# Two memories laid out by feature, parameters as one array, and the small inner products of eight units regrouped

## The chip, the cores and the metric

One core of a Trainium2 chip runs the whole program. The metric is the device time in microseconds (us) of one execution; the median of three runs stands for a kernel. TensorE (PE; its weight loads are PEld), VectorE (DVE), ScalarE (ACT), GpSimd (POOL) and SyncE (SP, which issues most DMAs) each run their own list of instructions in order and meet at semaphores.

## The reference

Two blocks of a sequence model, at batch 1, 256 tokens and 1024 features, all in float32. Block 1: an RMS norm and one wide projection feed a stick-breaking attention (sb), an mLSTM branch (ml) and a cross attention (xa) over 256 memory rows `mem`, whose norm is `mem * rsqrt(mean(mem^2)) * g_mem`; the gated outputs are merged and projected, and a convolved gated feed-forward follows. Block 2, two layers: a gated linear recurrence over 8 heads (hg, the part the change touches), a latent attention with rotary positions (mla), an attention over a second memory `mem_2` that is not normed, an output projection and a LayerNorm.

What the eight heads compute, in the form that the kernel uses: with `b` the running sum of the log forget gates,

```python
A[t, s] = sum_d q[t, d] * exp(b[t, d] - b[s, d]) * k[s, d]     # s <= t
o[t]    = sum_s A[t, s] * v[s]
```

The kernel forms `exp` of such differences about the midpoint of every node of a binary tree over the 256 tokens, so that each exponent is at most zero.

## The kernel before

Every float32 operand of a large product is split into an upper and a lower part. ACT copies a landed weight piece from `raw` (4 slots) to `whi` (6 slots, L1065), DVE subtracts to get `wlo` (L1538), and PE does three products for each tile: upper by upper, upper by lower, lower by upper (L589 to L591 where the output is by feature, L598 to L600 where it is by token). A piece is 512 KB of a weight matrix, 24 or 12 matmuls. Pieces stand in one list, and all engines go through it in order; `split_until(n)` in the ACT and DVE programs says up to which piece they split before their next other work, mostly six pieces ahead of PE. SP loads piece c when DVE has split piece c-4. `project(name, ...)` is PE's loop over the pieces of one matrix, `part` a range of them. The order of everything between pieces is written out by hand in each engine's program; there is no planner.

**The start.** SP loads the identity, `mem` in two row blocks, then pieces 0 to 3, then X. ACT issues 13 small DMAs of parameter vectors into staging rows. PE transposes three of these vectors (L675), DVE copies them to `cols1` (L1603), PE transposes `mem` in 16 tiles (`turn`, L634), ACT and DVE split the tiles from PSUM with the gain `g_mem` (`turned`, L1104 and L1559), and only then are the first weight pieces split and `xak`, the first projection, begins. The 16 transposes of the normed X come between `xak` and `xav`, those of the other parameters (L689 to L693) between `xav` and `xaq`. Row sums of squares of `mem` and X are ACT passes with an accumulator (L1154, L1160).

**The small constants.** After the evacuations of `xak` and `xav`, ACT copies the tree masks (L1179) and takes logs and sines (L1184, L1186), and DVE does some twenty-five small operations for the rotary angles (L1627 to L1654), before both go on with the pieces of `xaq`. In the attention of `xa`, DVE's `attend_shares` ends with the normed shares, ACT's `attend_turned` (L1117) copies their transposes, and PE's `attend_values` (L659) waits for these.

**The second memory.** `mem_2` is loaded twice by row block, each time transposed by PE in 16 tiles (before `out20`, and before `hgf0` of layer 0) and split by ACT and DVE tile by tile.

**The recurrence (in each of two layers).** Eight units u, two for each pair of heads. PE's `decays(u, ...)` sums logs through tree masks (L935, L936), ACT takes the exponential (`weights`, L1425), DVE multiplies keys and queries in (`factors`, four operations at L496), PE forms the inner products (`products`), DVE moves them into AT and AC (`keep`), and after an odd unit puts the diagonal blocks into AT (`diagonal`, L2027). Then PE can form the pair's outputs (`outputs`, L997, L998). An even unit has the levels of 128, 64 and 32 columns (L964, L968, L971) and level 3 in 32-column products (L979); an odd unit has levels 4 to 8, five levels in 32-column products (L979). `products(u-1)` stands in PE's program after `decays(u, 2, 4)`; a piece of `hgg` stands between `decays(u, 0, 2)` and `decays(u, 2, 4)`. After the last unit come `outputs(2)`, `products(7)`, a piece of `mlaout1`, `squares(2)` (L1004) and `outputs(3)`, which waits for DVE's `keep(7)`, `gated(2)`, `scaled(0)` and `diagonal(3)`.

**The end.** DVE adds the last projection to X by row block, takes its statistics, waits for ACT's square root, takes the reciprocal (L2094), then subtracts the mean and multiplies by the gain (L2095), and scales and adds (L2099).

## Time and profile before

| | us |
|---|---|
| median of three runs | 1051.24 (1051.14 to 1052.27) |
| profiled execution, its own time | 1052.53 |
| its span in the trace | 1050.7 |
| PE busy | 1030.6 |
| DVE busy | 730.9 |
| ACT busy | 654.1 |

The busy time of an engine is the union of its instructions. A matmul's end is modelled and overlaps the next one's start, so a PE that runs on steadily is seen best by the distance between starts, which is what the chain of waits prints. The mean granted clock over the span is 0.997. In the chain of waits the six projection lines have 13% of the span each, and PE as a whole has 95%.

### The profile page before, as it was taken

What the parts mean: (1) busy time and instruction counts of PE and PEld (TensorE: products, weight loads), DVE (VectorE), ACT (ScalarE), POOL (GpSimd) and SP (SyncE); (2) the same over time, 40 slices, a digit from 0 to 9 for tenths busy, and PEclk for the clock granted to TensorE, in tenths of its full rate; (3) what the DMA queues carried; (4) which work ended last, traced back from release to release, by engine and by line L of the source; (5) the groups of instructions that cost most, each with busy time, mean ns of one, the idle gap of its engine ahead of it and who ended that gap; (6) DMA issues with size and microseconds to landing.
All of it is one profiled execution on the core that took longest, in us unless ns stands there. A gap on an engine that the chain in (4) does not pass through costs nothing.

```text
span 1050.7 us, 19082 instructions
## 1 busy us (share of the span) xinstructions
PE 1030.6 (98%) x8048; PEld 922.0 (88%) x8048; DVE 730.9 (70%) x1085; ACT 654.1 (62%) x924; POOL 13.3 (1%) x18
## 2 busy tenths in 40 slices
PE   6999999999999999999999999999999999999996
PEld 5798987888989999988999998888799999988875
DVE  4684688885747788765565758977884656599686
ACT  6776576564456656544466678657755667776583
POOL 1000000000000000000000000100000000001000
PEclk9999999999999999999999999999999999999999
DMA  8663434666547655566544533422565455344231
GB/s 307 225 202 120 142 124 137 200 200 201 173 149 228 195 179 167 193 223 187 173 160 130 165 125 120 141 83 102 180 199 168 130 161 161 101 143 142 79 116 47
DMA packets 97831, 167.52 MB, mean 159 GB/s; under 512 B 7048, under 2 KB 32530, under 8 KB 97490
## 3 DMA queue, kind: packets, MB, share of 16 engines
q1 hardware_dynamic: 95776, 159.24, 47.3%
q0 software_dynamic: 1472, 5.51, 1.5%
q10 hardware_dynamic: 498, 1.55, 0.4%
q8 instruction: 63, 1.03, 0.4%
q14 instruction: 22, 0.18, 0.0%
HBM read 165.23 MB, written 1.05 MB: 158 GB/s over the span
## 4 chain that ended last, share of the span: by engine, by line
PE 95%; DVE 3%; DMA 1%; ACT 1%; issue 1%; SPq 0%; DVEq 0%
PE proj L598 13%; PE proj L589 13%; PE proj L600 13%; PE proj L599 13%; PE proj L591 13%; PE proj L590 13%; PE mix L935 1%; PE mix L979 1%; PE mix L936 1%; PE mix L634 1%; PE mix L659 1%; PE mix L642 1%; PE mix L968 1%; DVE wlo L1538 1%; DMA raw<-in_w_mem_kv 1%; PE mix L875 1%
## 5 line engine op out<-in xcount | busy, mean ns | idle before, releaser
L1538 DVE TENSOR_TENSOR wlo<-raw,whi 128x1024 fp32r<-128x1024 f32 (+3 forms) x303 | 355.4, 1202 | 139.9 <-ACT whi L1065 138.0
L1065 ACT ACTIVATE whi<-raw 128x1024 fp32r<-128x1024 f32 (+3 forms) x303 | 306.2, 1040 | 148.1 <-PE proj L600 66.5
L589 PE MATMUL proj<-act_hi,whi 128*128 128x256 f32 x1064 | 303.5, 285 | 0.6 <-ACT arena L1082 0.4
L591 PE MATMUL proj<-act_hi,wlo 128*128 128x256 f32 x1064 | 300.9, 283 | 0.0
L590 PE MATMUL proj<-act_lo,whi 128*128 128x256 f32 x1064 | 300.9, 283 | 0.0
L589 PEld LDWEIGHTS proj<-act_hi,whi 128*128 128x128 f32 x1064 | 203.1, 191 | 3.3 <-ACT arena L1082 1.2
L590 PEld LDWEIGHTS proj<-act_lo,whi 128*128 128x128 f32 x1064 | 203.2, 191 | 0.9
L591 PEld LDWEIGHTS proj<-act_hi,wlo 128*128 128x128 f32 x1064 | 203.2, 191 | 0.2
L598 PE MATMUL proj<-whi,y_hi 128*128 128x512 f32 (+1 forms) x340 | 135.1, 397 | 3.8 <-DVE wlo L1538 3.5
L599 PE MATMUL proj<-wlo,y_hi 128*128 128x512 f32 (+1 forms) x340 | 132.4, 389 | 0.0
L600 PE MATMUL proj<-whi,y_lo 128*128 128x512 f32 (+1 forms) x340 | 132.3, 389 | 0.0
L598 PE MATMUL proj<-whi,act_hi 128*128 128x512 f32 (+1 forms) x288 | 113.3, 393 | 0.0
L600 PE MATMUL proj<-whi,act_lo 128*128 128x512 f32 (+1 forms) x288 | 111.0, 386 | 0.0
L599 PE MATMUL proj<-wlo,act_hi 128*128 128x512 f32 (+1 forms) x288 | 110.9, 385 | 0.0
L598 PEld LDWEIGHTS proj<-whi,y_hi 128*128 128x128 f32 x340 | 64.3, 189 | 19.5 <-DVE wlo L1538 4.3
L600 PEld LDWEIGHTS proj<-whi,y_lo 128*128 128x128 f32 x340 | 64.3, 189 | 13.5
L599 PEld LDWEIGHTS proj<-wlo,y_hi 128*128 128x128 f32 x340 | 64.3, 189 | 12.7 <-issue 0.5
L598 PEld LDWEIGHTS proj<-whi,act_hi 128*128 128x128 f32 x288 | 54.1, 188 | 10.3 <-issue 0.5
L600 PEld LDWEIGHTS proj<-whi,act_lo 128*128 128x128 f32 x288 | 54.1, 188 | 10.2
L599 PEld LDWEIGHTS proj<-wlo,act_hi 128*128 128x128 f32 x288 | 54.1, 188 | 9.6
L1076 ACT ACTIVATE arena<-proj 128x1024 f32<-128x1024 f32 (+2 forms) x40 | 39.8, 996 | 36.4 <-PE proj L591 21.7
L496 DVE TENSOR_TENSOR arena<-arena 128x512 f32<-128x512 f32 x64 | 41.1, 703 | 25.9 <-ACT arena L1425 25.5
(360 smaller groups left out, 1239.7 us busy)
## 6 DMA issues: line engine op xcount, KB each, us to landing
raw<-in_w_in SPq DMA_DIRECT2D x144, 512.0 KB, 4.4
raw<-in_w_up SPq DMA_DIRECT2D x88, 256.0 KB, 4.2
raw<-in_w_out SPq DMA_DIRECT2D x32, 512.0 KB, 4.3
raw<-in_w_down SPq DMA_DIRECT2D x22, 512.0 KB, 5.4
raw<-in_w_mem_kv SPq DMA_DIRECT2D x8, 512.0 KB, 9.1
raw<-in_w_mem_k SPq DMA_DIRECT2D x8, 512.0 KB, 4.0
raw<-in_w_o SPq DMA_DIRECT2D x8, 512.0 KB, 3.7
raw<-in_w_mem_v SPq DMA_DIRECT2D x8, 512.0 KB, 3.9
```

The costliest lines, as they stand in the source:

```text
L496: return mul(z, z, kq, ALU.mult)
L589: mm(o, wh[:, i, wc], hi[:, k0 + i, :], start=begin and j % 2 == 0, stop=False, skip_group_check=True)
L590: mm(o, wh[:, i, wc], lo[:, k0 + i, :], start=False, stop=False, skip_group_check=True)
L591: last = mm(o, wl[:, i, wc], hi[:, k0 + i, :], start=False, stop=end, skip_group_check=True)
L598: mm(o, hi[:, k0 + i, tb], wh[:, i, :], start=begin, stop=False)
L599: mm(o, hi[:, k0 + i, tb], wl[:, i, :], start=False, stop=False)
L600: last = mm(o, lo[:, k0 + i, tb], wh[:, i, :], start=False, stop=end)
L634: last = nc.tensor.transpose(mix[:, k // 2, (k % 2) * SEQ + b * P:(k % 2) * SEQ + (b + 1) * P], src(k, b), ident)
L642: last = mm(mix[:, h, b * SEQ:(b + 1) * SEQ], q(h)[:, b * P:(b + 1) * P], k(h), start=True, stop=True)
L1065: fn(whi[c % SPLIT][:, 0:w], raw[c % SLOTS][:, 0:w], ACT.Copy).then_inc(s.w_hi, 1)
L1076: fn(dst, src, func).then_inc(out_of(name, L)[0], 1)
L1538: tt(wlo[c % SPLIT][:, 0:w], raw[c % SLOTS][:, 0:w], f32(whi[c % SPLIT][:, 0:w]), ALU.subtract).then_inc(s.w_lo, 1)
```

## The change

One diff with these parts. (1) On the host, arrays are laid out: `mem` and `mem_2` by feature, `[128, 8, 256]`, and all parameter vectors by column in one array `par`; the kernel loads `mem` in two halves of four feature tiles, and `par` in one DMA. (2) The transposes of `mem`, of `mem_2` (twice) and of the parameters are gone. ACT and DVE split `mem` straight from SBUF, and `mem_2` in one operation each. The sums of squares of `mem` are an ACT square, a DVE sum over the eight tiles, and two small matmuls with a vector of ones after `xak`. (3) The transposes of X stand between the second and third piece of `xav`. (4) The small constants move behind the first attention's exponentials. (5) The inner products: level 8 goes from the odd unit to the even one; an even unit is `outer_products`; an odd unit is `early_products` (levels 4, 5), which PE does a unit later between its two halves of `decays`, and `late_products` (levels 6, 7); for unit 7 the late ones come amid the piece of `mlaout1`. DVE copies the widest levels of an even unit (`keep_widest`) between the second and third of the odd unit's `factors`, and `early_products` wait for it. (6) In the last LayerNorm the subtraction comes ahead of the wait for the square root.

```diff
 # SP
-            sp.dma_start(const[:, 0:P], a["const"][:, 0:P]).then_inc(s.ident_in, 16)
-            for b in range(NB):
-                sp.dma_start(MEM[:, b, :], a["mem"][0, b * P:(b + 1) * P]).then_inc(s.mem_in, 16)
             for c, loads in enumerate(pieces):
-                if c == SLOTS:
+                if c in (0, 2):
+                    half = slice(c * KT // 4, c * KT // 4 + KT // 2)
+                    sp.dma_start(MEM[:, half, :], a["mem"][:, half, :]).then_inc(s.mem_rest if c else s.mem_in, 16)
+                if c == SLOTS + 1:
                     sp.dma_start(X[:, :, :], a["x"][0].rearrange("(b p) d -> p b d", p=P)).then_inc(s.x_in, 16)
...
 # PE, the start
+            project("xak", None, MEM_hi, MEM_lo, ready=lambda k: pe.wait_ge(s.mem_lo, k))
+            pe.wait_ge(s.mem_sum, 1)
+            for b in range(NB):
+                last = mm(mix[:, 3, 4 * b:4 * b + 4], MEM_SUM[:, b * P:(b + 1) * P], ONE4, start=True, stop=True)
+            last.then_inc(s.mem_ss, 1)
+            project("xav", None, MEM_hi, MEM_lo, part=(0, 2))
+            pe.wait_ge(s.norm_x, 1)
             pe.wait_ge(s.ident_in, 16)
...
-            turn(KT, lambda k, b: MEM[:, b, k * P:(k + 1) * P])
-            project("xak", None, MEM_hi, MEM_lo, ready=lambda k: pe.wait_ge(s.mem_lo, k))
-            pe.wait_ge(*stage(2, None))
-            pe.wait_ge(s.norm_x, 1)
-            turn(KT, lambda k, b: XN[:, b, k * P:(k + 1) * P])
-            project("xav", None, MEM_hi, MEM_lo)
...
 # PE, the second memory (the same in layer 0)
-            pe.wait_ge(s.mem2_in, 16)
-            turn(KT, lambda k, b: MEM2_AT[None][:, b, k * P:(k + 1) * P])
...
 # PE, the inner products
+                def outer_products(u):
+
+                    pe.wait_ge(s.hg_z, 32 * L + 4 * u + 4)
+                    if u:
+                        pe.wait_ge(s.hg_cp, 8 * L + u)
+                    else:
+                        pe.wait_ge(s.hg_ll, 4 * L + 4)
+                    inner(u, (8,))
...
+                    inner(u, (3,)).then_inc(s.hg_pr, 1)
+
+                def early_products(u):
+
+                    pe.wait_ge(s.hg_z, 32 * L + 4 * u + 2)
+                    pe.wait_ge(s.hg_outer, 4 * L + u // 2 + 1)
+                    inner(u, (4, 5))
+
+                def late_products(u):
+
+                    pe.wait_ge(s.hg_z, 32 * L + 4 * u + 4)
+                    pe.wait_ge(s.hg_cp, 8 * L + u)
+                    inner(u, (6, 7)).then_inc(s.hg_pr, 1)
...
                 for u in range(1, UNITS):
                     decays(u, 0, 2)
+                    if u % 2 == 0:
+                        early_products(u - 1)
...
-                    products(u - 1)
+                    if u % 2:
+                        outer_products(u - 1)
+                    else:
+                        late_products(u - 1)
...
+                early_products(UNITS - 1)
                 outputs(2)
-                products(UNITS - 1)
-                project("mlaout1", L, y_hi, y_lo, 8, part=(1, 2))
+                project("mlaout1", L, y_hi, y_lo, 8, part=(1, 2), amid=lambda: late_products(UNITS - 1))
...
 # ACT
+            act.dma_start(par[:, :], a["params"]).then_inc(s.params, 16)
+            act.dma_start(const[:, 0:P], a["const"][:, 0:P]).then_inc(s.ident_in, 16)
...
+            mem_upper(range(KT // 2))
+            split_until(2)
+            act.wait_ge(s.mem_rest, 16)
+            mem_upper(range(KT // 2, KT))
+            split_until(SLOTS)
+            fn(MEM_SQ, MEM, ACT.Square).then_inc(s.mem_sq, 1)
...
             attend_exp(0, XP, XA_D ** -0.5)
+            split_until(ahead_of("sbv", None, 1))
             act.wait_ge(s.tree_in, 16)
             fn(tree[:, :, :, :].rearrange("p b l t -> p (b l t)"), TREE_IN, ACT.Copy).then_inc(s.tree_ok, 1)
...
-            turned("mem2", None, KT, MEM_hi, lambda k: 1.0)
+            act.wait_ge(s.mem2_in, 16)
+            fn(MEM_hi, MEM2_AT[None], ACT.Copy).then_inc(s.mem2_hi, 1)
...
 # DVE
+                    stt(MEM_lo[:, k, :], MEM[:, k, :], cols1[:, 1, k:k + 1], f32(MEM_hi[:, k, :]), ALU.mult, ALU.subtract).then_inc(s.mem_lo, 1)
...
                     for i in range(4):
-                        last = halves(tt, u, i)
-                    last.then_inc(s.hg_z, 1)
+                        if u % 2 and i == 2:
+                            keep_widest(u - 1)
+                        halves(tt, u, i).then_inc(s.hg_z, 1)
+
+                def keep_widest(u):
+
+                    heads = slice(u, u + 2)
+                    dve.wait_ge(s.hg_pr, 8 * L + u + 1)
+                    if u == 0:
+                        dve.wait_ge(s.hg_zero, L + 1)
+                    copy(AT[:, heads, P:SEQ], mix[:, 2, 0:SEQ].rearrange("p (h t) -> p h t", h=2))
+                    copy(both(AT[0:64, heads, 64:P], SEQ, 64), mix[0:64, 2, SEQ:512].rearrange("p (h b t) -> p h b t", h=2, b=2)).then_inc(s.hg_outer, 1)
...
+                        link(masked(3, mix[:, 3, P:2 * P]))
+                        last = masked(8, mix[:, 3, 2 * P:3 * P])
...
+                    stt(x, x, stat[:, 72 + 2 * b:73 + 2 * b], LNG, ALU.subtract, ALU.mult).then_inc(s.ln_s, 1)
                     dve.wait_ge(s.ln_r, 2 * L + b + 1)
                     nc.vector.reciprocal(r, r).then_inc(s.ln_s, 1)
-                    stt(x, x, stat[:, 72 + 2 * b:73 + 2 * b], LNG, ALU.subtract, ALU.mult).then_inc(s.ln_s, 1)
```

## Rows read from the trace of the kernel before

**Rows 1.** the page's busy times: engine, us busy, share of the span, instructions.

```profile
PE 1030.6 (98%) x8048; PEld 922.0 (88%) x8048; DVE 730.9 (70%) x1085; ACT 654.1 (62%) x924; POOL 13.3 (1%) x18
```

**Rows 2.** PE's waits over the span: what waited, for what, us, times, longest.

```profile
PE proj L598 <- DVE wlo L1538: 3.5, 2, 2.3
...
PE mix L979 <- issue: 0.8, 2, 0.5
```

**Rows 3.** the timeline at the start: start us, us, engine, line, operation.

```profile
6.38 3.56 PE L634 MATMUL mix<-const,arena 128*128 128x128 f32 x16 [0.68 <-DMA arena<-in_mem]
7.57 1.63 ACT L1104 ACTIVATE y_hi<-mix,cols 128x256 fp32r<-128x256 f32 x4 [0.64 <-PE mix L634]
```

**Rows 4.** the chain of waits, first 41 us: start us, us, what.

```profile
9.84 1.06 ACT whi L1065
...
12.21 0.50 PE proj L598
...
17.06 0.23 PE proj L599
...
39.30 0.41 PE mix L689 x5
...
40.31 0.43 PE proj L598
```

**Rows 5.** busy time by stretch: PE, PEld, DVE, ACT, POOL, granted clock, DMA share, GB/s.

```profile
6.00:7.00 1.00, 0.62 (x3) 0.66 (x4) 0.00 (x0) 0.92 (x1) 0.00 (x0) 1.00 0.73 203
13.00:14.00 1.00, 1.00 (x4) 0.80 (x3) 0.96 (x4) 1.00 (x2) 0.00 (x0) 0.56 1.00 397
16.00:17.00 1.00, 1.00 (x5) 0.82 (x4) 0.51 (x1) 1.00 (x2) 0.28 (x1) 0.73 0.67 211
```

**Rows 6.** the timeline of PE about the second memory's transposes.

```profile
224.69 1.91 PE L634 MATMUL mix<-const,arena 128*128 128x128 f32 x16
226.35 0.48 PE L598 MATMUL proj<-whi,y_hi 128*128 128x512 f32 x1
```

**Rows 7.** the timeline of PE, inner products of units 1 and 3, layer 0.

```profile
682.78 0.40 PE L936 MATMUL mix<-tree_r,y_lo 128*128 128x512 f32 x1
683.11 1.56 PE L979 MATMUL mix<-arena 128*32 128x32 f32 x160
684.60 0.50 PE L935 MATMUL mix<-tree_r,y_hi 128*128 128x512 f32 x1
684.94 0.40 PE L936 MATMUL mix<-tree_r,y_lo 128*128 128x512 f32 x1
...
702.59 1.46 PE L979 MATMUL mix<-arena 128*32 128x32 f32 x149
704.54 0.32 PE L979 MATMUL mix<-arena 128*32 128x32 f32 x11 [0.48 <-issue]
```

**Rows 8.** the timeline of PE behind the last unit, layer 1.

```profile
1017.62 0.70 PE L997 MATMUL mix<-arena 128*128 128x256 f32 x2
```

**Rows 9.** the timeline of DVE behind the last two units, layer 1.

```profile
1011.41 0.41 DVE L2008 COPY arena<-mix 128x256 f32<-128x256 f32 x1
1011.74 0.40 DVE L2009 COPY arena<-mix 64x256 f32<-64x256 f32 x1
...
1013.85 1.65 DVE L2005 COPY_PREDICATED arena<-const,mix 128x128 f32<-128x128 uint32 x5 [0.88 <-PE mix L979]
...
1016.66 0.91 DVE L2027 COPY arena<-arena 32x128 f32<-32x128 f32 x4
```

**Rows 10.** the timeline of ACT, small constants and first attention.

```profile
43.11 1.91 ACT L1179 ACTIVATE tree_r<-arena 128x2048 fp32r<-128x2048 f32 x1
...
91.51 2.06 ACT L1117 ACTIVATE arena<-mix 128x512 f32<-128x512 f32 x4
```

**Rows 11.** the timeline of PE, first attention's value products.

```profile
92.15 3.72 PE L659 MATMUL mix<-arena 128*128 128x256 f32 x16
```

**Rows 12.** the chain of waits, last 15 us.

```profile
1040.80 1.19 DVE X L2095
```

More of the change, by code:

```diff
@@ L85, with by_column, laid_out @@
 PI = 3.1415925
+def by_column(*rows):
+    return np.concatenate([v.reshape(-1, P).T for v in rows], 1)
+PARAM_NAMES = {"block1": ("g_mix", "g_mem", "g_ffn", "ml_conv_w", "ml_conv_b"), "ffn": ("ff_conv_w", "ff_conv_b"),
+               "heads": ("xa_g_q", "xa_g_k", "hgrn_out_norm_2", "mla_q_norm_2", "mla_kv_norm_2"), "logits": ("hgrn_lb_logits_2",)}
+PARAMS = {"block1": 0, "ffn": 8 * KT, "heads": 8 * KT + 8 * FT, "logits": 8 * KT + 8 * FT + 10,
+          "bias": 10 * KT + 8 * FT + 10, "end": 10 * KT + 8 * FT + 18}
+def laid_out(inputs):
+    named = {name: np.asarray(inputs[name]) for name in _INS}
+    arrays = {name: np.ascontiguousarray(named[name]) for name in _WHOLE}
+    bias = np.concatenate([named["ml_b_i"][0], named["ml_b_f"][0]])
+    columns = [by_column(*(named[name] for name in names)) for names in PARAM_NAMES.values()]
+    arrays["params"] = np.ascontiguousarray(np.concatenate([*columns, np.broadcast_to(bias, (P, 2 * ML_H))], 1))
+    for name in ("mem", "mem_2"):
+        arrays[name] = np.ascontiguousarray(named[name][0].T.reshape(KT, P, SEQ).transpose(1, 0, 2))
+    arrays["positions"] = np.ascontiguousarray(named["positions_2"][0].reshape(NB, P).T)
+    arrays["const"], arrays["tree"] = CONST, TREE
+    return arrays
 def piece(w, row, k, col, n):
@@ L198, in __init__ @@
         self.trig_a = new("trig_a")
+        self.mem_rest = new("mem_rest")
+        self.mem_hi = new("mem_hi")
         self.mem_lo = new("mem_lo")
+        self.mem_sq = new("mem_sq")
+        self.mem_sum = new("mem_sum")
+        self.mem_ss = new("mem_ss")
+        self.mem2_hi = new("mem2_hi")
         self.x_lo = new("x_lo")
@@ L286, in __init__ @@
         self.hg_cp = new("hg_cp")
+        self.hg_outer = new("hg_outer")
         self.hg_at = new("hg_at")
@@ L374, in cst @@
             return const[:, b:e]
+        cols1 = par[:, PARAMS["block1"]:PARAMS["ffn"]].rearrange("p (v k) -> p v k", k=KT)
+        cols2 = par[:, PARAMS["ffn"]:PARAMS["heads"]].rearrange("p (v k) -> p v k", k=2 * FT)
+        cols3 = par[:, PARAMS["heads"]:PARAMS["logits"]]
+        logits = par[:, PARAMS["logits"]:PARAMS["bias"]].rearrange("p (v k) -> p v k", k=KT)
+        rowbias = par[:, PARAMS["bias"]:PARAMS["end"]]
         ident, ones = cst("ident"), cst("ones")
@@ L559, in _, with project @@
             mm = nc.tensor.matmul
-            def project(name, L, hi, lo, tile0=0, ready=None, part=None, half=None):
+            def project(name, L, hi, lo, tile0=0, ready=None, part=None, half=None, amid=None):
                 g, ps, at = place[L, name], shape[L, name], number[L, name]
@@ L602, in project @@
                                 last.then_inc(half, 1)
+                            if amid is not None and b == 0:
+                                amid()
                     last.then_inc(s.w_used, 1)
@@ L1145, in _, with mem_upper @@
             nc.scalar.preload_act_table(ACT.Copy)
-            act.wait_ge(*stage(1, None))
-            turned("mem", None, KT // 2, MEM_hi, lambda k: cols1[:, 1, k:k + 1])
-            split_until(1)
-            turned("mem", None, KT // 2, MEM_hi, lambda k: cols1[:, 1, k:k + 1], KT // 2)
-            split_until(2)
-            FIRST_SS, FIRST_R = stat[:, 232:236], stat[:, 236:240]
+            def mem_upper(tiles):
+                for k in tiles:
+                    fn(MEM_hi[:, k, :], MEM[:, k, :], ACT.Copy, scale=cols1[:, 1, k:k + 1]).then_inc(s.mem_hi, 1)
@@ L1155, in _ @@
             link(last)
-            split_until(SLOTS)
-            act.wait_ge(s.x_in, 16)
-            act.dma_start(const[:, P:], a["const"][:, P:]).then_inc(s.consts, 16)
-            for b in range(NB):
-                last = fn(XN[:, b, :], X[:, b, :], ACT.Square, accum_out=FIRST_SS[:, 2 + b:3 + b])
-            link(last)
-            rsqrt(FIRST_R, FIRST_SS, DM, EPS, None).then_inc(s.norm_r, 1)
-            split_until(SLOTS + 1)
+            split_until(SLOTS + 2)
+            fn(FIRST_R[:, 2:4], FIRST_SS, ACT.Ln, bias=epsb[:, 0:1], scale=1.0 / DM)
@@ L1165, in leave_mem @@
+            act.wait_ge(s.mem_ss, 1)
+            link(fn(FIRST_R[:, 0:2], mix[:, 3, 0:8].rearrange("p (b c) -> p b c", c=4)[:, :, 0], ACT.Ln, bias=epsb[:, 0:1], scale=1.0 / DM))
+            fn(FIRST_R, FIRST_R, ACT.Exp, scale=-0.5).then_inc(s.norm_r, 1)
+            split_until(pieces_until("xak", None))
             def leave_mem(name, dst):
@@ L2007, in keep @@
                     if u % 2 == 0:
-                        copy(AT[:, heads, P:SEQ], mix[:, 2, 0:SEQ].rearrange("p (h t) -> p h t", h=2))
-                        copy(both(AT[0:64, heads, 64:P], SEQ, 64), mix[0:64, 2, SEQ:512].rearrange("p (h b t) -> p h b t", h=2, b=2))
                         for n in range(2):
```

235 lines of the change are left out of this document (97 added, 138 removed).

## The prediction

> **What bounds the kernel now.** I read the page's busy times first: PE is busy for 98% of the span, ACT and DVE have a third of it to spare [rows 1]. So I count only what PE executes and what it waits for. PE's waits are few: 3.5 us for split weight pieces in two waits, the longer of 2.3 us ahead of the first projection, the other (1.2 us) behind the transposes of X, and two pauses of 0.8 us together inside runs of small products that no semaphore explains [rows 2]. The chain of waits then gives three stretches in which PE does something else than projections, and these are what the change touches: the start up to 12.21, the units' small products, and the LayerNorm after PE's last matmul [rows 4, 7, 12]. A projection step of 512 columns costs 0.23 us from start to start [rows 4].
>
> **1. The start.** Before, ACT starts on piece 0 at 9.84 and PE's first projection matmul starts at 12.21, 2.37 us later [rows 4]. Ahead of that stand the transposes of `mem`, from 6.38 on, and ACT's split of four tiles, 1.63 us [rows 3]. After the change ACT can split the first four tiles as soon as the half memory and the parameters are there. PE waited for the whole memory until 6.38 [rows 3]; a half in one DMA at the head of the queue I put at 4.6, between 4.0 and 5.3 (an estimate: half the bytes, the same latency). Then 4.6 + 1.6 + 2.4 = 8.6 for the first matmul, with bounds of 7.8 and 10.5, the latter if piece 0 lands late beside the parameters, as it did when ACT could only start it at 9.84. That is 3.6 us earlier.
>
> Part of it goes to the clock. The 16 transposes at 6.38 took 3.56 us [rows 3], the same 16 later take 1.66 [rows 6], so PE began slow, although the granted clock reads 1.00 there [rows 5]. PE was then fast at 12.21, and the granted clock fell to 0.50 (1.2 GHz) within the second 13 to 14 after an idle stretch and rose again within 16 to 17 [rows 5]: about 3.4 us slow, 1.7 us lost. After the change PE starts with projections and nothing before them. If it stays slow for 3.4 to 6.8 us it loses 1.7 to 3.4; I take 2.3, that is 0.6 more than before. The Trainium skill (TensorE: Matmul & The Clock Gate, Part 1: The HAM clock gate) says that the slow clock is the default and sustained work releases it. By that page the transposes' pace is to be believed and the granted 1.00 of rows 5 is not; by the column the new start would lose nothing and the sum would be 2.3 lower.
>
> The transposes of the parameters go: from 39.30 to 40.31 plus 0.2 for the slow step behind them, 1.2 us [rows 4]. The two matmuls for the sums of squares come in, 0.35 (as the similar small transposes, between 0.2 and 0.6). The wait of 1.2 us behind the transposes of X goes, with 0.1 beside it, as these now stand ahead of two pieces (5.5 us of PE), while DVE's two tile sets and one piece take 4.6 us; what is late next is piece 9, behind ACT's evacuation of `xak`, with some 2 us in hand. On the DMA queues 13 small loads become one, X moves one piece back, the tables' loads (1.4 MB and 1 MB) move far behind their old place; all are needed tens of us later. Sum for the start: -3.6 + 0.6 - 1.2 + 0.35 - 1.4 = **-5.3** (bounds -7.5 and -2.5).
>
> **2. The second memory.** Each set of 16 transposes costs PE 1.66 us up to the next start and 0.08 to 0.17 of a slow step [rows 6]; I take 1.83 with the pace of the chain. Twice: **-3.7**. ACT and DVE do one operation of 2048 columns instead of eight, less work. No new wait: neither is near its use (in layer 1, which has no such transposes, PE does not wait at that place either).
>
> **3. The small constants.** They now stand on ACT between the attention's exponentials and `attend_turned`. From the tree copy at 43.11 (1.91 us) two table loads and five small passes follow, 5.3 us in all, and two pieces are split behind them. Before, the copies of the shares started at 91.51 and PE's value products at 92.15, right when the first copy was done [rows 10, 11]. With ACT's earlier idle stretches used up I get 92.4 for that start, so **+0.8** (0 to 2).
>
> **4. The inner products.** 160 records (80 products) of 32 columns run from 683.11 to 684.60. The step before would have ended at 683.01, and the next step is 0.34 instead of 0.23 [rows 7]. Of these 1.70 us the products are 1.38, at 8.6 ns a record, and entering and leaving the narrow shape is 0.32. The change adds, for each pair of heads, one such entry and exit by the split into early and late, and one by putting level 8 ahead of the 128-column products: 16 in all, 16 x 0.32 = **+5.2**. The products themselves are as many as before. At the least the entry alone (0.1) is paid, 1.6.
>
> The pauses inside two runs in layer 0 (702.59 with 149 records, then idle 0.48 us) cost 0.7 us each against the undisturbed run [rows 7]. Runs of 64 records end before the points, record 149 and 92, at which those stopped, so I take **-1.4**. The Trainium skill (Runtime: NRT & Kernel Launch, Instruction fetch mechanics) says that fetching is mostly hidden because PE issues slower than it fetches. By that page these pauses are not of fetching, and nothing says that shorter runs lose them; the sum would be 1.4 higher.
>
> New waits. `early_products` wait for DVE's `keep_widest`, which waits for the even unit's last product. For units 1, 3 and 5 the first half of `decays` (0.9 us) lies between. For unit 7 nothing does: the end of the last product (0.2), two copies (0.33 + 0.4 [rows 9]) and the semaphores are 1.0 us on PE. Queued behind `keep_widest` on DVE are two of the four factors, `keep(6)` and all else; `late_products(7)` needs both, but a full `outputs(2)` and half a piece lie between. Then `outputs(3)`. Before, DVE's five masked copies began at 1013.85 and the last of `diagonal` ended at 1017.57; `outputs(3)` started at 1017.62, so it was just not waiting [rows 8, 9]. Now PE has half of the piece less to do behind the last product, 1.38 us, and pays 0.2 more in shapes; DVE has one masked copy (0.31) less. Wait: about 1.0. Together 1.9 a layer, **+3.8** (0 to 5). For the first pair DVE is busy throughout, and standing still at `keep_widest` for 1.3 us makes `outputs(0)` late: I allow 0.3 a layer, **+0.6** (0 to 2).
>
> **5. The end.** The subtraction of 1.19 us [rows 12] starts 0.35 earlier, beside the square root. DVE is the chain there for both row blocks: **-0.7**.
>
> **Sum**: -5.3 - 3.7 + 0.8 + 5.2 - 1.4 + 3.8 + 0.6 - 0.7 = -0.7. The profiled execution took 1052.5 (a span of 1050.7 and 1.8 around it), so 1051.8; the median of the runs is 1.3 below the profiled one, and 0.7 below the median is **1050.5**.
>
> **The rivals.** (a) The narrow shape is cheap. Its price of 0.32 is read where a run stands between 512-column steps; part of it is a step whose end the profile models. If a run only costs the entry, 0.1, part 4 loses 3.5 and the time is **1047.0**. For it: the pace inside a run is even. Against: the next start really is 0.11 late [rows 7]. (b) DVE stands still. `keep_widest` sits in the middle of `factors`, and DVE's queue waits there for PE's even run at every pair, not only the last; behind it wait the late factors, `keep` and the weight splits. It decides once DVE's slack at a pair is under the 1.3 us of that stand; then each of the three other pairs of a layer costs PE about 0.7 instead of 0.1: 6 x 0.6 = +3.6, so **1054.1**. For it: at the first pair DVE has no slack. Against: later pairs have DVE idle for microseconds. (c) The change does not do what it says to the pauses: they come wherever PE runs through instructions fast, and stay. 1050.5 + 1.4 = **1051.9**.
>
> **How the numbers follow.** No change can be told within 0.2% (2.1 us, 1049.1 to 1053.3). Forecast 0.45, of it 0.39 within, 0.04 faster, 0.02 slower; (a), or as much more at the start, 0.30, nearly all faster; (b) 0.17, nearly all slower; (c) 0.08, within. So faster 0.32, same 0.47, slower 0.21. The likeliest case alone spans 1048.5 to 1052.5; the range takes in (a) and most of (b): 1046.8 to 1054.3.
>
> **What would show it.** PE's first projection matmul at 8.6 (not over 10.5), slow steps of 0.43 from there; no wait at the transposes of X; `xaq` starting near 35. 16 more entries into L979-like runs, each 0.1 before and 0.1 to 0.2 behind; PE waiting for DVE's copies ahead of the last unit's early products and of `outputs(3)`, about 1 us each and in both layers. Were these waits absent and the shapes free, (a) is right; were PE to wait for DVE at every pair, (b). I would be wrong altogether if PE waited at the start for pieces or for `mem` beyond 10.5.

## The result and the profile after

The changed kernel takes 1056.6 us (median of 4, 1056.5 to 1057.0), the kernel before on the same chip 1051.5 (4 executions, 1051.1 to 1052.3): ratio 1.004, interval 1.0028 to 1.0053. It is 0.4 to 0.5% slower. The forecast was 1050.5 us with a range up to 1054.3: wrong, and in sign. The profiled execution took 1056.7 with a span of 1054.9, 4.2 more than the span before. Against [rows 1] PE is as busy as before:

```profile
PE 1030.6 (98%) x7990; PEld 916.8 (87%) x7990; DVE 733.0 (69%) x1067; ACT 654.7 (62%) x909; POOL 11.3 (1%) x15
```

To place the 4.2 us I set PE's matmuls of the two timelines side by side by their source line and followed the difference of their starts (after minus before). It stands at -3.2 at the first attention's transposes, -3.1 at its value products and up to 183 us, -1.5 at 191, -3.3 behind the first removal of the second memory's transposes, -4.5 behind the second, -0.4 at the end of layer 0's recurrence, +4.9 at the end of layer 1's, and the tail takes 0.7 off. Six terms, and each is read below.

**The start.** PE's timeline (start us, us, engine, line, operation), to be set beside [rows 3, 4]:

```profile
10.51 0.80 PE L627 MATMUL proj<-whi,y_hi 128*128 128x512 f32 x1 [10.51 <-DVE wlo L1572]
11.11 0.63 PE L628 MATMUL proj<-wlo,y_hi 128*128 128x512 f32 x1
11.53 0.63 PE L629 MATMUL proj<-whi,y_lo 128*128 128x512 f32 x1
...
15.80 0.43 PE L627 MATMUL proj<-whi,y_hi 128*128 128x512 f32 x1
16.07 0.40 PE L628 MATMUL proj<-wlo,y_hi 128*128 128x512 f32 x1
```

and ACT's, which splits the first weights:

```profile
5.54 1.70 ACT L1173 ACTIVATE y_hi<-arena,par 128x256 fp32r<-128x256 f32 x4 [2.59 <-DMA par<-in_params]
8.14 1.06 ACT L1100 ACTIVATE whi<-raw 128x1024 fp32r<-128x1024 f32 x1 [0.90 <-DMA raw<-in_w_mem_kv]
```

The halved memory and the parameters are there at 5.5, the first piece of weights (piece 0) only at 8.1, and ACT stands still for it. It did so before too, in the kernel whose transposes I took for the limit:

```profile
9.84 1.06 ACT L1065 ACTIVATE whi<-raw 128x1024 fp32r<-128x1024 f32 x1 [0.65 <-DMA raw<-in_w_mem_kv]
```

So the start was bound by the landing of piece 0 before and after, and the first matmul comes 1.7 us earlier because ACT can start on the piece 1.7 us earlier (8.14 for 9.84). From there the chain is the old one, 2.4 us to the first matmul at 10.51. Its steps are 0.43 us apart until 15.8 and 0.23 after that: the slow clock, 12 steps x 0.2 = 2.4 us.

**The low clock at 183 us.** The kernels do the same there, yet after the change the difference grows by 1.6 us. Busy time by stretch (PE, PEld, DVE, ACT, POOL, granted clock, DMA share, GB/s):

```profile
182.00:183.00 1.00, 1.00 (x5) 0.59 (x5) 1.00 (x1) 0.98 (x2) 0.00 (x0) 1.00 0.81 299
183.00:184.00 1.00, 1.00 (x5) 0.77 (x4) 1.00 (x5) 0.99 (x2) 0.00 (x0) 0.57 0.85 303
184.00:185.00 1.00, 1.00 (x4) 0.81 (x3) 1.00 (x4) 0.98 (x2) 0.00 (x0) 0.50 0.89 279
185.00:186.00 1.00, 1.00 (x4) 0.81 (x3) 0.76 (x3) 0.99 (x2) 0.00 (x0) 0.50 0.99 373
186.00:187.00 1.00, 1.00 (x4) 0.72 (x4) 0.00 (x0) 1.00 (x1) 0.00 (x0) 0.73 1.07 410
```

The granted clock goes to 0.50 (1.2 GHz) for 3.4 us, and PE's chain shows what precedes it (L784 are the products that spread four rows to 128) and what it does to the steps:

```profile
180.80 1.83 PE mix L784 x8
182.63 0.43 PE proj L627
183.06 0.26 PE proj L628
183.31 0.43 PE proj L629
183.74 0.43 PE proj L627
```

In the profiled execution of before the clock stayed at 1.00 there. That the changed start brings the low clock is not shown: the kernel with the old start and the new products alone, below, has it at 187 us too.

**The recurrences.** PE's waits over the whole span (what waited, for what, us, times, longest), beside [rows 2]:

```profile
PE mix L1025 <- DVE arena L2071: 2.1, 2, 1.0
PE mix L974 <- DVE arena L2037: 1.9, 2, 1.0
```

The pauses of [rows 2, 7] are gone; in their place PE waits, once in each layer, for `keep_widest` ahead of the last unit's early products, and for `diagonal(3)` ahead of `outputs(3)`. PE's timeline behind layer 1's last unit, where [rows 8] had `outputs(3)` at 1017.62 without a wait:

```profile
1013.25 0.46 PE L974 MATMUL mix<-arena 128*32 128x32 f32 x30
1014.67 0.75 PE L974 MATMUL mix<-arena 128*32 128x32 f32 x64 [0.96 <-DVE arena L2037]
...
1018.25 0.76 PE L974 MATMUL mix<-arena 128*32 128x32 f32 x64
1018.94 0.50 PE L627 MATMUL proj<-whi,y_hi 128*128 128x512 f32 x1
...
1022.49 0.70 PE L1025 MATMUL mix<-arena 128*128 128x256 f32 x2 [1.04 <-DVE arena L2071]
```

DVE's timeline shows what the second wait waits through: the masked copies end at 1020.37, then come two operations of the gate, then the diagonal's copies. The two gate operations stood there before as well, at 1015.40 and 1016.00 between the copies of [rows 9]. What is new is PE's side: from the end of the last narrow run to `outputs(3)` it had 3.9 us of work before (1013.74 to 1017.62) and has 2.5 now (1018.94 to 1022.49 less the wait of 1.04).

```profile
1019.05 1.32 DVE L2049 COPY_PREDICATED arena<-const,mix 128x128 f32<-128x128 uint32 x4 [2.02 <-PE mix L974]
1020.27 0.68 DVE L2078 TENSOR_TENSOR arena<-proj,arena 128x512 f32<-128x512 f32 x1
1020.87 0.74 DVE L2084 SCALAR_TENSOR_TENSOR arena<-arena,cur 128x512 f32<-128x512 f32 x1
1021.53 0.91 DVE L2071 COPY arena<-arena 32x128 f32<-32x128 f32 x4
```

### The profile page after: what moved, and what is told of

Same layout as the page of the kernel before. It is cut to its first block, busy times and chain, and to the rows that moved or that the text cites. A ratio compares the mean times of both kernels' runs of the same rounds, so it can differ in the third digit from the quotient of the medians.

```text
span 1054.9 us, 18921 instructions
## 1 busy us (share of the span) xinstructions
PE 1030.6 (98%) x7990; PEld 916.8 (87%) x7990; DVE 733.0 (69%) x1067; ACT 654.7 (62%) x909; POOL 11.3 (1%) x15
## 3 DMA queue, kind: packets, MB, share of 16 engines
q8 instruction: 63, 1.03, 0.4%
## 4 chain that ended last, share of the span: by engine, by line
PE 94%; DVE 3%; ACT 1%; issue 1%; DMA 1%; SPq 0%; DVEq 0%
PE proj L627 13%; PE proj L618 13%; PE proj L629 13%; PE proj L628 13%; PE proj L620 13%; PE proj L619 13%; PE mix L974 1%; PE mix L947 1%; PE mix L948 1%; PE mix L665 1%; PE mix L690 1%; PE mix L673 1%; PE mix L992 1%; PE mix L887 1%; DVE wlo L1572 1%
## 5 line engine op out<-in xcount | busy, mean ns | idle before, releaser
L627 PE MATMUL proj<-whi,y_hi 128*128 128x512 f32 (+1 forms) x340 | 136.4, 401 | 11.4 <-DVE wlo L1572 10.5
L627 PEld LDWEIGHTS proj<-whi,y_hi 128*128 128x128 f32 x340 | 65.0, 191 | 27.3 <-DVE wlo L1572 10.5
L628 PEld LDWEIGHTS proj<-wlo,y_hi 128*128 128x128 f32 x340 | 65.0, 191 | 12.8 <-issue 0.5
```

The lines of the kernel that those rows point to most:

```text
L627: mm(o, hi[:, k0 + i, tb], wh[:, i, :], start=begin, stop=False)
L628: mm(o, hi[:, k0 + i, tb], wl[:, i, :], start=False, stop=False)
```

## The experiments

The chips differed from one set of runs to the next, and the kernel before spread over 1051.5 to 1056.5 us in them. So each kernel is told with the median of before in its own set.

### First set (before: 1053.6)

**Old products in the changed rest.** `inner`, `outer_products`, `early_products` and `late_products` give way to `products(u)` as it was; factors, copies and waits too.

```
-                    if u % 2:
-                        outer_products(u - 1)
-                    else:
-                        late_products(u - 1)
+                    products(u - 1)
```

> The changed kernel with the units' inner products put back as they were (one run of 32-column products per unit, level 8 with the odd unit, the widest levels copied in the unit's copy and not amid the factors); all else as changed. Theory A (the products carry the loss): the changed trace stands +9.4 us later over the two recurrences (+4.1 in layer 0, +5.3 in layer 1), so this kernel should take 1056.6 - 9.4 = 1047.2 us, and its trace should still show the low granted clock at 182.9 to 186.5 us, which lies before any product. Rival B (the products cost what was taken from the widest single terms only, the rest is drift that any shift of the timeline brings): only the 16 additional entries go, 1056.6 - 5.2 = 1051.4 us.

Measured: 1055.2 us (1052.0 to 1058.7), ratio 1.0015 (1.0003 to 1.0026). Neither theory. PE's waits name the reason:

```profile
PE mix L990 <- issue: 6.9, 4, 2.5
```

The products are those of before, where this row was 0.8 us in two [rows 2]. PE's timeline at unit 5 of layer 0:

```profile
718.43 1.46 PE L990 MATMUL mix<-arena 128*32 128x32 f32 x148
721.34 0.32 PE L990 MATMUL mix<-arena 128*32 128x32 f32 x12 [1.44 <-issue]
721.58 1.13 PE L1015 MATMUL proj<-arena,const 128*128 128x512 f32 x2
```

No semaphore explains it, but the queues do. Within 718.9 to 719.0 one packet of 16 KB stands on a queue of the kind "instruction" (queue, kind: packets, MB, share):

```profile
q8 instruction: 1, 0.02, 56.4%
```

PE goes on 2.4 us later. In the four pauses of this kernel the packet came at 679.65, 718.95, 732.95 and 1013.15, and PE went on at 681.98, 721.34, 735.37 and 1015.80: 2.3 to 2.65 us each time. The two pauses of before fit as well: packets at 702.25 and 731.65, on at 704.54 and 734.09. Over its span the changed kernel has

```profile
q8 instruction: 63, 1.03, 0.4%
```

and 1.03 MB over its 7990 matmuls and 7990 weight loads are some 64 bytes each, so a packet of 16 KB holds about 256 instructions of PE's code (an estimate; waits at semaphores are not counted in it). A run of 160 narrow matmuls is 320 instructions in 1.5 us, while PE went on 2.3 us or more behind a packet. A packet within a run is not enough for a pause: in unit 3 of layer 1 one comes 1.3 us into the run, and PE does not stop. Behind the longest pause the granted clock falls, in stretches of 2 us of this kernel:

```profile
732.00:734.00 2.00, 0.89 (x107) 0.77 (x93) 0.08 (x1) 1.98 (x3) 0.00 (x0) 1.00 0.03 8
734.00:736.00 2.00, 0.63 (x8) 0.59 (x9) 0.30 (x1) 1.69 (x2) 0.00 (x0) 0.88 0.00 0
736.00:738.00 2.00, 2.00 (x6) 1.52 (x6) 1.87 (x6) 0.00 (x0) 0.00 (x0) 0.50 0.00 0
```

**The new products alone**, in the kernel before.

```
-                    products(u - 1)
+                    if u % 2:
+                        outer_products(u - 1)
+                    else:
+                        late_products(u - 1)
...
```

> The kernel before with the changed inner products alone (parameters, memories, start and norm as before). Theory A (the parts add up): 1051.5 + 9.4 = 1060.9 us, no low clock near 186 us, since the timeline up to the recurrence is that of before, clock column 0.997. Rival B (the parts do not add up: the loss needs the shifted start or the new memory layout): about 1051.5 + 5.2 = 1056.7 us or less.

Measured: 1063.2 us, ratio 1.0091 (1.0076 to 1.0107), 9.6 above its before where 9.4 were forecast. The parts add up. The low clock did come in its profiled execution, at 187 and at 736 us, so that part of the expectation is wrong. At 736 no pause stands ahead of it, only PE's wait of 0.96 us for `keep_widest`, so a long pause is not the only thing that the low clock there can follow.

**Narrow runs joined.**

```
-                    inner(u, (8,))
...
-                    inner(u, (3,)).then_inc(s.hg_pr, 1)
+                    inner(u, (8, 3)).then_inc(s.hg_pr, 1)
...
                     else:
+                        early_products(u - 1)
                         late_products(u - 1)
```

> The changed kernel with its narrow runs joined, everything else and the copies amid the factors kept: level 8 goes into the run of level 3 behind the wide products, levels 4 and 5 directly ahead of 6 and 7 at the later place (for the last unit both within the projection's piece). So each pair has two narrow runs and not four, 16 fewer entries and exits. Theory A (each entry and exit costs about 0.32 us, and the last unit's early run waits 1.0 us a layer for the widest copies): 1056.6 - 5.2 - 2.0 = 1049.4 us, up to 1.4 us more if the pauses within long runs come back (1050.8), and up to 0.6 more where outputs(3) waits longer. Rival B (entries are cheap, the cost lies in DVE's copies amid the factors, which this kernel keeps): 1054 us or more.

Measured: 1050.8 us (1048.3 to 1051.5), ratio 0.997 (0.9958 to 0.9982). Beside the changed kernel's trace it gains 2.7 us over layer 0's recurrence and 3.1 over layer 1's, 5.8 where 7.2 were forecast; one pause of 0.24 us came back in a run of 128. The low clock at 183 us is missing in its trace, and that is another 1.3. Theory A with a smaller size.

**PE busy from 1 us on**, by 14 products on memory that DVE sets to zero.

```
...
+            pe.wait_ge(s.warm_in, 1)
+            for _ in range(14):
+                mm(mix[:, 0, 0:256], arena[:, 0:128], arena[:, 0:256], start=True, stop=True)
             project("xak", None, MEM_hi, MEM_lo, ready=...)
```

> The changed kernel with 14 products of 256 columns on a zeroed piece of memory, in fp32, ahead of the first projection, so that TensorE is busy from about 1 us on; its results are overwritten. Theory A (the 0.43 us steps from 11.1 to 15.8 us are the slow clock, which follows an idle engine): the steps are 0.23 us from the first one, about 11 steps x 0.20 = 2.2 us less: 1054.4 us; and if the shift also takes the low clock at 183 us away, 1.6 less still, 1052.8 us. Rival B (the first steps are bound by the landing of pieces): the engine waits for pieces in place of slow steps, 1056.6 us.

Measured: 1052.7 us, ratio 0.9994 (0.9985 to 1.0002). The steps are fast from the start:

```profile
1.19 8.23 PE L706 MATMUL mix<-arena 128*128 128x256 f32 x28 [1.19 <-DVE arena L1637]
10.29 0.50 PE L628 MATMUL proj<-whi,y_hi 128*128 128x512 f32 x1 [0.87 <-DVE wlo L1576]
10.63 0.40 PE L629 MATMUL proj<-wlo,y_hi 128*128 128x512 f32 x1
10.87 0.40 PE L630 MATMUL proj<-whi,y_lo 128*128 128x512 f32 x1
11.11 0.40 PE L628 MATMUL proj<-whi,y_hi 128*128 128x512 f32 x1
```

At 15.8 us of the old timeline it is 2.6 ahead, and behind 187 us 4.2, since the low clock did not come in this execution. Three of the eleven executions took 1054.0 to 1054.3 us at a mean clock of 0.996, so it was not gone for good. One pause of 0.23 us came directly behind the last unit's early run, 2.4 us after a packet: the changed products are not free of them. Theory A.

### Second set (before: 1053.1)

**Before again**, unchanged, for its profile.

> The kernel before, unchanged, for its profile beside the others. On the chip of the last four it spread over 1051.6 to 1056.5 us. Theory A (pauses of fetched code: in the traces read so far TensorE resumes 2.3 to 2.65 us after a 16 KB packet of the instruction queue, and only inside runs of 160 narrow matmuls): each pause in its runs of 160 ends 2.3 to 2.7 us after such a packet, and two to four of its eight odd units have one. Rival B (pauses come from the data: banks, semaphores): pauses stand at no fixed distance from such packets.

One execution: 1051.2 us. One pause, 0.49 us in unit 3 of layer 0, at matmul 149 as in [rows 7], 2.3 us behind its packet: fewer than A expected, and where A wants it. Its first projection matmul came at 11.76 and all its steps were 0.23 us apart: the low clock of [rows 5] at 13 us did not come. That moved the start by 1.0 us at 45 us of the timeline: the changed kernel, 3.2 ahead of the first trace of before, is 2.2 ahead of this one.

**The changed kernel again.**

> The changed kernel, unchanged, so that the others can be set against it on one chip. Theory A: no pause inside its narrow runs, none being longer than 64 matmuls, and a narrower spread than before; 1056.6 us, or 1.6 less where the low clock at 183 us does not come (1055.0). Rival B (the first four times were of one chip's conditions): its spread is as wide as that of before.

Measured: 1054.8 us (11 executions), ratio 1.0021 (1.0011 to 1.0031). The executions fall into two groups: six of 1053.6 to 1054.8 us with a mean granted clock of 0.998, five of 1055.9 to 1057.2 with 0.996. The profiled one is of the second, with the low clock from 181.9 on. All four of the first result had 0.996. No pauses; but its spread of 3.6 us is that of before (3.3), so the narrower spread of A did not come.

**Code shifted.** The old products in the changed rest, 128 instructions later, in PE's idle time.

```
+            for n in range(32):
+                j = n % 4
+                mm(mix[32 * j:32 * j + 32, 0, 0:32], arena[:, 0:32], arena[:, 0:32], start=True, stop=True)
             project("xak", None, MEM_hi, MEM_lo, ready=...)
```

> The kernel with the old products in the changed rest (its four pauses, 0.68 to 2.48 us, came at matmul 146, 148, 153 and 120 of a run of 160), with 32 products of 32 columns on a zeroed piece at the very start, while TensorE waits for its first weights: 64 matmuls and 64 loads, 128 instructions, so that every later instruction stands 8 KB further on. Theory A (the pauses are the fetching of code, 16 KB at a time): each pause moves 64 matmuls towards the start of its run (146 to 82, 148 to 84, 153 to 89, 120 to 56), or comes in another run, and still ends 2.3 to 2.65 us after its packet. Rival B (a cause in the data or in the bank): the pauses stay at 146, 148, 153 and 120.

Measured: 1045.8 us, ratio 0.9935 (0.992 to 0.9951). PE's waits and the only pause:

```profile
PE mix L995 <- issue: 0.3, 1, 0.3
```

```profile
697.85 1.45 PE L995 MATMUL mix<-arena 128*32 128x32 f32 x146
699.55 0.33 PE L995 MATMUL mix<-arena 128*32 128x32 f32 x14 [0.26 <-issue]
```

Its packet came at about 697.2, ahead of the run, and PE went on 2.4 us after it. The positions 146, 148, 153 and 120 kept no pause, against B. One of A's new positions has a pause in the trace: unit 7 of layer 0, stopped at 153 without the shift, stops at 89 for 0.12 us. At 82, 84 and 56 nothing stops; in units 1 and 5 the nearest packet comes 4.5 and 5.5 us ahead of the run and none inside it, so there PE had the block in time. Two later kernels with the same shift had 0.3 and 0.5 us of such pauses, so the size stays with the place. 6.9 us of pauses became 0.3, and the low clock behind the last of them went too. In one set with the changed kernel, this is the price of the new products with almost no pauses on the other side: 1054.8 - 1045.8 = 9.0 us.

**Joined and busy from 1 us on.**

> The changed kernel with joined narrow runs and with the 14 products on zeros at the start, the two edits together. Theory A (independent gains: 4.2 us less for the start and the low clock at 183 us, about 5.8 us less over the recurrences by the trace with joined runs): 1056.6 - 2.6 - 5.8 = 1048.2 us, and 1.6 less again against runs of the changed kernel that have the low clock. Rival B (the joined runs of 128 are long enough for pauses): up to 2 us more, and a wider spread than the changed kernel's.

Measured: 1047.8 us, ratio 0.995 (0.9936 to 0.9963). That is A's figure, in part by luck: it was taken from 1056.6, and against the changed kernel of the same set (1054.8) the two edits gain 7.0 us where 8.4 were forecast. The low clock came in its trace too, at 180 us.

### Third set (before: 1053.4)

**The changed kernel shifted**, with the same 32 products at its start.

> The changed kernel, products as changed, with the same 32 narrow products on zeros at the start as in the kernel with shifted code: 128 instructions more. Theory A (the shift acts only through pauses in runs of 160 matmuls, which the changed kernel does not have): no difference to the changed kernel, 1054.8 us (1053.6 to 1057.2 as its executions were). Rival B (the products at the start or the shift help by themselves): about as much as the shift gave the old products, 5 to 9 us less.

Measured: 1056.2 us (1053.9 to 1057.1), ratio 1.0025 (1.0015 to 1.0034). 1.4 us above A's figure but, against before of its own set, as the changed kernel (1.0021): neither the shift nor the products at the start do anything by themselves in it.

**Level 8 in the run of level 3**, one edit of the joined kernel alone.

> The changed kernel with one edit: level 8 goes into the run of level 3 behind the wide products, so 8 narrow runs fewer; no wait is touched. Theory A (0.32 us for each entry and exit): 8 x 0.32 = 2.6 us less, 1054.8 - 2.6 = 1052.2 us, and in the trace some 0.3 us at each pair. Rival B (a narrow run has no price of its own beyond its matmuls): no difference.

Measured: 1051.7 us (1051.3 to 1054.3), ratio 0.9992 (0.9983 to 1.0002). Beside the timeline of a kernel with the runs as changed (the last one of the fourth set), it gains 0.28 to 0.32 us at each of the eight pairs: the price of a narrow run, as forecast. Against the changed kernel (shifted) of the same set it took 4.4 us less where 2.6 were forecast; the low clock at 183 us, absent in this trace and present in the other, accounts for 1.6 of it.

**Shifted and busy from 1 us on**: the old products, and the 128 additional instructions are products of 128 rows and 112 columns.

> The old products in the changed rest, code shifted by the same 128 instructions, but these are 32 products of 128 rows and 112 columns that keep TensorE busy until the first weights are there. Theory A (the slow clock of the start and the pauses are independent): 1045.8 - 2.6 = 1043.2 us. Rival B (the start is bound by the landing of weights): 1045.8 us.

Measured: 1043.4 us (1042.5 to 1044.1), ratio 0.9907 (0.9894 to 0.9921). Theory A to 0.2 us, and the fastest kernel here, 0.9% below before and 12.8 us below the changed kernel (shifted) of the same set.

**Thin products apart.**

```
             for h in range(ML_H):
+                if h == 2:
+                    project("out00", None, y_hi, y_lo, 4, part=(0, 1))
                 last = mm(mix[:, h // 2, ...], pick[0:4, h, :], ROWS[0][0:4, :], start=True, stop=True)
```

> As the kernel before it in this list (shifted and busy from the start), with the eight matmuls of four rows that stand ahead of the low clock at 183 us (180.80 to 182.63 us in the changed kernel's trace) set apart: four, a piece of the output projection (about 3 us), four. Theory A (the clock falls there because 2 us of matmuls that use four of 128 rows count as little work): no execution has the low clock there, and the times have one group, at the lower end of the other's. Rival B (the clock falls by chance of time, whatever stands there): low clock as often as in the other.

Measured: 1045.3 us over four executions (a fifth took 2044 us, which nothing here explains; with it the median is 1045.6). Inconclusive on the clock: the kernel it is set against had mean clocks of 0.998 and 0.999 in all its executions, so it had no low clock there to lose. It is 1.9 us slower, of which 1.1 are a new wait of PE for DVE some 12 us later.

### Fourth set (before: 1053.7)

**Shift of 64 and of 192 instructions**, with 16 and 48 narrow products at the start.

> The old products in the changed rest, with 16 narrow products on zeros at the start, 64 instructions more (a quarter of a block of 256). Without a shift the blocks ended at matmul 146, 148, 153 of runs of 160 and the pauses came to 6.9 us; with 128 instructions to 0.3 us. Theory A (position in the code): the ends move to about matmul 114, 116, 121 and 88, nearer to the start of the run, so that the fetch starts earlier against it: pauses of some 3 us in all, 1048 to 1050 us. Rival B (chance of the execution, not position): the time is as that of the kernel without a shift or with 128, with a wide spread that covers both, 1045 to 1056 us.

> The same with 48 narrow products, 192 instructions more. Theory A: the ends that stood at 146, 148 and 153 come to about 50 to 57 and give no pause; other runs' ends move into their last third; about 1045 to 1048 us, and executions within 3 us of each other. Rival B: as for the shift of 64.

Measured: 1047.0 us for 64 (1045.7 to 1048.0, ratio 0.9942) and 1053.8 for 192 (1052.4 to 1055.8, ratio 1.0005). PE's waits, first with 64, then with 192:

```profile
PE mix L995 <- issue: 1.0, 3, 0.4
```

```profile
PE mix L995 <- issue: 7.3, 3, 2.6
```

So over a block of 256 instructions the same work takes 1.6 us more than before, 6.7 less, 7.3 less and 0.1 more. Position rules, against B; but A's sizes were wrong at both places: for 64 it had some 3 us of pauses and 1048 to 1050 us, and for 192 no long ones and 1045 to 1048 us. Its positions were right to the matmul where PE stopped at all. With 64 instructions more, unit 7 stops at 121 in layer 0 and at 88 in layer 1, 32 matmuls ahead of the 153 and 120 without a shift, as forecast:

```profile
727.88 1.23 PE L995 MATMUL mix<-arena 128*32 128x32 f32 x121
729.49 0.55 PE L995 MATMUL mix<-arena 128*32 128x32 f32 x39 [0.38 <-issue]
```

With 192 more, layer 1's unit 7 stops at 152, which is 120 - 96 + 128: the next block's end, 128 matmuls and their 128 loads further on. That is the length of a block, read from the stops themselves.

The three pauses with 192, 2.30 to 2.63 us, stand in layer 1; the longest:

```profile
998.86 1.46 PE L995 MATMUL mix<-arena 128*32 128x32 f32 x148
1002.96 0.32 PE L995 MATMUL mix<-arena 128*32 128x32 f32 x12 [2.63 <-issue]
```

with the packet at 1000.6, 0.3 us after PE had stopped: the bad place had moved from layer 0's runs to layer 1's.

**Before shifted** by 128 instructions.

> The kernel before with the same 32 narrow products ahead of its first transposes (128 instructions more), in its idle time. Theory A (the kernel before stands at a position where the pauses come to only 0.5 to 0.8 us): another position can only bring up to 1 us, and may cost several: between 1052.5 and 1058 us. Rival B (the kernel before loses as much to pauses as the old products in the changed rest did): it gains 5 us or more, 1048 us.

Measured: 1063.4 us (1060.4 to 1067.6), ratio 1.0101 (1.0077 to 1.0125), more than A allowed. PE's waits and its unit 5 of layer 0:

```profile
PE mix L984 <- issue: 7.9, 4, 2.7
```

```profile
724.59 1.50 PE L984 MATMUL mix<-arena 128*32 128x32 f32 x152
728.75 0.34 PE L984 MATMUL mix<-arena 128*32 128x32 f32 x8 [2.67 <-issue]
```

The kernel before stood at a lucky place. Not all of it is pauses: by the traces the shifted copy stands 1.4 us later at 45 us already, as its first projection matmul comes 0.3 us later and its steps are slow (0.43 us apart), and two of its pauses are followed by the low clock. Against before of its own set it loses 9.7 us, the changed kernel 1.7 and (shifted) 2.7: beside the shifted copy of before the change would have looked like a gain of some 7 us (across sets, each against its own before).

**Full products between the thin ones.**

```
             for h in range(ML_H):
+                mm(mix[:, 3, 256:512], tri[:, 0, 0:P], tri[:, 0, :], start=True, stop=True)
                 last = mm(mix[:, h // 2, ...], pick[0:4, h, :], ROWS[0][0:4, :], start=True, stop=True)
```

> The changed kernel with a product of 128 rows and 256 columns on constants (two matmuls of 0.23 us) ahead of each of the four products of four rows at 181 us; its results are not used. It costs 8 x 0.23 = 1.8 us by itself. Theory A (the low clock follows the 1.83 us of matmuls of four rows): no execution has the low clock at 183 us any more, so all stand at 1053.9 + 1.8 = 1055.7 us in one group. Rival B (it comes by chance of time): two groups, 1055.7 and 1058.3 us.

Measured: 1057.9 us. The inserted products cost 3.2 us in the trace, not 1.8. Two groups remain: 1056.8, 1057.8 and 1057.9 (clock 0.998 to 0.999), 1059.2 and 1059.7 (0.996). The kept trace is of the first group and has no low clock; that the second had it at 183 us is taken from the mean clock alone. Nothing speaks for theory A; what makes the clock fall at 183 us in some executions stays open.

## Why the prediction was wrong, step by step

| term | forecast | measured |
|---|---|---|
| start | -5.3 | -3.2 |
| small constants | +0.8 | +0.1 |
| low clock at 183 us | none | +1.6 |
| second memory | -3.7 | -3.0 |
| inner products, all parts | +8.2 | +9.4 |
| end | -0.7 | -0.7 |
| sum | -0.7 | +4.2 |

The 4.9 us between the sums and the 1.3 us by which the profiled execution of before lay above its median (that of after did not) make the 6.1 us of the miss.

- **Start.** The step that failed is "4.6 + 1.6 + 2.4 = 8.6 for the first matmul". It let ACT turn to piece 0 when the memory's tiles were split, at 6.2. They were split at 7.2 (the memory and the parameters came at 5.5, not 4.6), and the piece landed only at 8.1; it had been issued behind half the memory. The same misreading stands in "as it did when ACT could only start it at 9.84": ACT was not held up by the transposes there, it had waited 0.65 us for the piece. The first matmul came 1.7 us earlier instead of 3.6, and these 1.9 us are nearly all of the term's miss of 2.1. The bound of 10.5 named this case and is what came. The slow clock was sized rightly (2.3, measured 2.4), and the kernel busy from 1 us on shows it to be avoidable. The granted clock reads 1.00 while steps take 0.43 us, so the steps are to be believed. There the rule of the Trainium skill (TensorE: Matmul & The Clock Gate, Part 1: The HAM clock gate), that the slow clock is the default, agrees with the trace.
- **Small constants.** Nothing became late. The cover that I thought used up was still there.
- **Low clock at 183.** No term: the second step that failed, put at nothing. The profile of one execution of before cannot show it; by the trace it is worth 1.6 us, and the changed kernel's own two groups, about half of its executions each, lie 2.5 apart. How often before has it there is not known.
- **Second memory.** Right for the first removal (1.8); the second brought 1.2, and where the other 0.6 went was not traced.
- **Entries and exits.** Right: 0.32 forecast, 0.28 to 0.32 at each pair where level 8 was joined. That refutes rival (a).
- **Last unit's waits.** Right in place and size: 4.0 us of waits for 3.8. Rival (b) is refuted: PE waits for DVE at the last unit alone, not at every pair. The third miss is the 1.2 us by which the products' 9.4 exceed the 8.2; it was not traced to a row.
- **Pauses.** For the kernel measured, right in kind: the two pauses went, and rival (c) did not come. They were worth 1.2 us against undisturbed runs (the runs took 2.26 and 2.10 us instead of 1.56), 1.4 was booked. In weight it was wrong. I read two pauses as the size of the effect, where they were the lucky draw: 0.3 to 7.9 us by where the code lies. The Trainium skill (Runtime: NRT & Kernel Launch, Instruction fetch mechanics) has the blocks of 256 instructions on a queue of the engine's own, as the trace shows, and calls crossing them "mostly hidden"; here it is not, up to 2.67 us a crossing.

Two slips of the prediction's own adding up move nothing by more than 0.1 us or 0.02: part 1 has 1.2 and 0.1 for the wait behind the transposes of X in its text and 1.4 in its sum, and the cases with their shares give at most 0.19 for slower, not 0.21.

What the change was worth is thus two answers. Its products cost 9.0 us against old products that hardly pause (one set, code shifted by 128 instructions) and remove pauses that were 0.3 to 7.9 us by where the code lay; unshifted, where the old products paused for 6.9 us, the two traces end only 2.0 us apart. At none of the four places was the changed rest with the old products slower (ratios to before 0.9935 to 1.0015) than the changed kernel (1.0021 to 1.0040), though at the unshifted place the intervals overlap.

## What to carry to other kernels

A run of hundreds of tiny matmuls has two prices that busy time does not show: some 0.3 us for entering and leaving, and a pause whose size hangs on the position of the code. Look at the instruction queue's packets beside each "issue" pause, shift the code by a quarter block at a time in idle time and measure, before judging any edit nearby, since each edit ahead of the run shifts it too. When the start is moved forward, follow the landing of every load of the first operation, and look in the old trace which engine already waits for one of them.

## What the runs showed of the hardware

- PE resumed 2.2 to 2.7 us after a 16 KB instruction packet in all 22 pauses of 0.2 us or more behind its start that the traces hold, in ten kernels; the old products' pauses came to 6.9, 1.0, 0.3 and 7.3 us for shifts of 0, 64, 128 and 192 instructions. What sets the moment at which a packet is asked for was not settled: 0.3 to 1.1 us before the run in most of the short pauses, 1.1 to 1.8 us into it in the eight of more than 2 us.
- Of the eight pauses of 2.2 to 2.7 us, four have the granted clock fall to 0.50 for 3.4 us, from 0.4 us before their end to 1.5 us behind it, so that they cost more than themselves; at the other four, one of 2.63 us among them, it did not fall.
- The stops mark the ends of the blocks of code: 153, 121 and 89 matmuls into one run for 0, 64 and 128 instructions more, and 92 and 156 in the kernel before without and with 128 more.
- 14 products of zeros at the start (8.2 us of otherwise idle PE) are worth 2.6 us.
- A sum over the outer of two dimensions (DVE, 2048 elements a partition, read with a stride) took 3.91 us, three times a split of 1024 elements by DVE.
